# Expert passes of 32 token slots on four column tiles, and one more part of the weights loaded ahead

## The chip, the cores and the metric

One core of a Trainium2 chip runs the whole program. The metric is its time on the device in microseconds (us), launched once with all inputs in the chip's memory. TensorE does the matrix products in fp32 out of the on-chip memory (128 rows) into eight accumulator banks of 128 rows by 512 fp32. VectorE and ScalarE do the elementwise work and read the banks. SyncE (SP) issues the large DMA transfers.

## What is computed

One block with attention, a Fourier mix and a mixture of experts, and behind it two layers with other mixers and plain MLPs, for 256 tokens of width 1024. The part around the change is the mixture of experts:

```
def moe(h, w_router, b_router, w_gate, b_gate, w_up, b_up, w_down, b_down):
    logits = jnp.dot(h, w_router, preferred_element_type=jnp.float32) + b_router
    top_logit, top_idx = lax.top_k(logits, TOP_K)          # 4 of 32 experts
    gates = jax.nn.softmax(top_logit, axis=-1)
    ...
        g = jnp.minimum(xb @ w_gate[e] + b_gate[e], SWIGLU_LIMIT)
        u = jnp.clip(xb @ w_up[e] + b_up[e], -SWIGLU_LIMIT, SWIGLU_LIMIT)
        act = g * jax.nn.sigmoid(SWIGLU_ALPHA * g) * (u + 1)
        return act @ w_down[e] + b_down[e]
```

The result for each token is the sum over its four experts, weighed by the gates. Each of the 32 experts has three matrices of 1024 x 1024 fp32, 12.6 MB, 403 MB in all. How many tokens an expert gets depends on the data. For the inputs of this case the reference's router gives, from expert 0 to 31:

```
22 29 25 37 37 5 12 32 47 41 54 24 25 51 35 13 28 55 32 30 68 10 39 41 23 39 36 36 33 21 11 33
```

With 64 tokens to a pass that is one pass for each expert and two for expert 20, 33 in all. With 32 tokens to a pass, and 64 for expert 31, it is 16 experts with one pass, 14 with two, expert 20 with three, and one pass of 64 for expert 31: 48.

## The kernel before

The program has three stages, each a block in which every engine runs its own instruction list and waits on semaphores: `stage_first` (attention, Fourier mix, router), `stage_experts`, and `stage_second` (the two further layers). A stage begins when all engines have ended the one before.

**Passes.** `stage_experts` goes through a list of passes that the router has written: `m.table` holds each expert's first pass, `m.keys` and `m.gates` the slot and the gate of each token in each pass. `SLOTS` is the number of tokens to a pass, 64. A pass treats the 1024 output columns as two halves, one on the array's columns 0 to 63 and one on 64 to 127 (two column tiles), so that both halves' matmuls run side by side: the stationary operand is a 128 x 64 piece of the tokens, the moving one 512 columns of weights. TensorE's list in `one_pass` is: `expand(G)` with w_gate (8 row blocks), `gather` of the next pass's tokens by a one-hot matrix `sel`, `expand(U)` with w_up, `turn_x` (transposes of the gathered tokens), transposes of the weighed one-hot matrix `selg`, `combine` of the previous pass's result y into four accumulator banks, transposes of the activation g, `biases` for the next pass, and the contraction with w_down (8 row blocks) into bank Y. VectorE computes u and g from the banks (L1529 to L1536), ScalarE the sigmoid and the copies out of the banks (L1496 to L1507). The loop over an expert's passes (`pe.Fori`, L1465) has bounds that TensorE's sequencer reads from the table (L1296).

**Weights.** An expert's weights are six parts of 2 MB (two each of w_gate, w_up, w_down; k = 0 to 5). The buffer `ring` has ten places for parts; part 6e+k goes to place (6e+k) mod 10, and may be written when the part ten before it has been used in the last pass of its expert (`used`, waits on w_free and down_ps). SP issues the parts in that order (L1334). Ten parts, those of expert 0 and four of expert 1, are loaded in `stage_first` (`load_ahead`). Behind the last expert's parts SP issues four loads for the next stage (L1356 to L1361), and in `stage_second` w columns (L1893), the toeplitz rows (L1899) and more.

**Clock.** `keep_busy` (L136) issues matmuls without use while TensorE would wait.

Of the kernel before, what the change touches and what calls it, by code (L numbers as in the profile page):

```python
# [11 lines left out]
ALU = mybir.AluOpType  # L12
# [18 lines left out]
SLOTS = 64  # L31
# [31 lines left out]
for _name, _n in (("ident", P), ("ones", P), ("tri", QT * SEQ), ("iota", P), ("causal", QT * SEQ), ("cmpvalid", QT), ("etri", EXPERTS), ("gate16", 16), ("pad", 6),  # L63
# [8 lines left out]
def shape_constants():  # L72
# [56 lines left out]
    put("etri", (e[:, None] < e[None, :]).astype(np.float32))  # L129
    return out, buckets  # L130
# [82 lines left out]

def load_ahead(sp, m, t, e, parts):
    for k in parts:
        q, _ = expert_part(e, k)
        sp.dma_start(part_rows(m, q), expert_rows(t, e, k)).then_inc(m.part_in[q], 16)


def stage_first(nc, m, t):  # L220
# [9 lines left out]
    m.sel = m.moe.sb("sel", [P, QT, SLOTS])  # L230
    m.now = m.moe.sb("now", [2 * EXPERTS, SLOTS])
# [76 lines left out]
    modb_in = {a: m.sem(f"modb_in{a}") for a in (0, 4, 8, 16)}  # L308
    m.toeplitz_out, m.brows_in = m.lasting("toeplitz_out"), m.lasting("brows_in")
# [44 lines left out]
    gate_rows = [m.selT[SLOTS * half:SLOTS * half + EXPERTS, :, :].rearrange("e i n -> e (i n)") for half in range(2)]  # L354
# [5 lines left out]
    with nc.Block() as block:  # L360
# [10 lines left out]
        def _(sp):  # L371
# [55 lines left out]
            load_ahead(sp, m, t, 0, (4,))  # L427

        @block.tensor
        def _(pe):  # L430
# [317 lines left out]
            pe.wait_ge(more_chain, 5)  # L748
# [10 lines left out]
            pe.wait_ge(more_chain, 9)  # L759
# [5 lines left out]
            pe.wait_ge(more_chain, 10)  # L765
# [6 lines left out]
            pe.wait_ge(turned_sb, 4)  # L772
# [5 lines left out]
        def _(act):  # L778
# [192 lines left out]
            for half in range(2):  # L971
                act.copy(gate_rows[half], ps[0:EXPERTS, 4, SEQ:2 * SEQ]).then_inc(turned_sb, 1)

        @block.vector
        def _(v):
# [243 lines left out]
            v.tensor_copy(more[:, 0:1], ps[0:EXPERTS, 5, 0:1])  # L1219
            v.tensor_copy(more[:, 3:4], ps[0:EXPERTS, 5, 1:2]).then_inc(more_chain, 1)  # L1220
            v.wait_ge(more_chain, 1)
            v.tensor_scalar(more[:, 1:2], more[:, 0:1], float(SLOTS), 1.0, ALU.is_gt, ALU.add).then_inc(more_chain, 1)
            for n in range(2, SEQ // SLOTS):
                v.wait_ge(more_chain, n)
                v.scalar_tensor_tensor(more[:, 1:2], more[:, 0:1], float(n * SLOTS), more[:, 1:2], ALU.is_gt, ALU.add).then_inc(more_chain, 1)
            v.wait_ge(more_chain, SEQ // SLOTS)
            v.sem_inc(more_chain, 1)
# [6 lines left out]
            v.tensor_copy(more[:, 2:3], ps[0:EXPERTS, 5, 2:3]).then_inc(more_chain, 1)  # L1234
            v.wait_ge(more_chain, 6)
# [31 lines left out]

def stage_experts(nc, m, t):

# [1785 lines left out]
```

## Time and profile before

| | us |
|---|---|
| median of three runs (lowest, highest) | 1847.85 (1847.38, 1848.78) |
| the profiled execution | 1845.13 |
| its span | 1843.3 |
| expert passes, first to last matmul of weights | 221.4 to 1128.2 |
| `stage_second` from | 1131.15 |

The profile is of one execution and times count from the span's start. PE is TensorE's matmuls, PEld its weight loads, DVE VectorE, ACT ScalarE, POOL GpSimd; a q behind a name is that engine's sequencer. An fp32 matmul of the program appears as two records. The profile has the granted share of TensorE's full clock (2.4 GHz); its mean is 0.996. "Landing" is the time from the issue of a transfer to its last byte.

### The profile page before, as it was taken

Reading aid. Unit: us, or ns where it says so; the run is one execution under the profiler, and the core shown is the slowest. Engines: PE = TensorE matmul, PEld = TensorE weight load, DVE = VectorE, ACT = ScalarE, POOL = GpSimd, SP = SyncE. Lnnn points to the kernel's source line nnn. Section 1 sums busy time; section 2 is a strip of 40 time slices with the busy share of each in tenths; the row PEclk is TensorE's granted clock in tenths of the full one; section 3 lists DMA queues with packets and bytes.
Section 4 is the critical chain, followed back from the end, with each engine's and each line's share of the span. In section 5 each row is a group of like instructions: output and inputs, shape, how many; then the busy total and the mean of one; then the engine's idle time right before and its main releaser. Section 6 shows DMA issues by size and latency. Waiting matters only on the chain. (4 is left out here: it accounts for less than half of the span.)

```text
span 1843.3 us, 23681 instructions
## 1 busy us (share of the span) xinstructions
PE 1799.4 (98%) x9487; PEld 1003.5 (54%) x9488; DVE 605.5 (33%) x1262; ACT 371.8 (20%) x721; POOL 10.9 (1%) x14
## 2 busy tenths in 40 slices
PE   7999899999999999999999999999999999999998
PEld 6757533333333333333333335767995466699843
DVE  1854411111111011011011013544655544345555
ACT  3222411111111111111111113332220033222101
POOL 0000000000000000000000000000000000000001
PEclk9999999999999999999999999999999999999999
DMA  9996699999999999999999999432446443124452
GB/s 379 390 191 271 261 418 430 431 431 431 432 432 431 432 431 431 432 431 432 431 431 431 432 431 329 156 142 92 151 149 241 160 182 137 46 92 149 149 176 98
DMA packets 104495, 558.61 MB, mean 303 GB/s; under 512 B 17128, under 2 KB 33997, under 8 KB 78701
## 3 DMA queue, kind: packets, MB, share of 16 engines
q1 hardware_dynamic: 101876, 553.06, 74.3%
q10 hardware_dynamic: 2554, 4.63, 1.8%
q8 instruction: 47, 0.77, 0.2%
q14 instruction: 18, 0.15, 0.0%
HBM read 552.43 MB, written 5.23 MB: 303 GB/s over the span
## 5 line engine op out<-in xcount | busy, mean ns | idle before, releaser
L1402 PE MATMUL ps<-ring,xs 128*64 128x512 f32 x2112 | 465.5, 592 | 4.9 <-DMA ring<-in_w_up 2.5
L1402 PEld LDWEIGHTS ps<-ring,xs 128*64 128x64 f32 x2112 | 151.3, 137 | 307.6 <-issue 298.2
L1456 PE MATMUL ps<-ring,actT 128*64 128x512 f32 x1056 | 233.9, 595 | 0.0
L2274 PE MATMUL ps<-ring 128*128 128x512 f32 x448 | 192.8, 592 | 0.0
L1529 DVE TENSOR_SCALAR hT<-ps 128x512 f32<-128x512 f32 x33 | 22.8, 692 | 446.0 <-PE ps L1402 446.0
L1456 PEld LDWEIGHTS ps<-ring,actT 128*64 128x64 f32 x1056 | 72.9, 137 | 158.7 <-issue 136.8
L2274 PEld LDWEIGHTS ps<-ring 128*128 128x128 f32 x448 | 84.9, 190 | 105.7 <-issue 105.7
L2010 PE MATMUL ps<-hT,ring 128*128 128x256 f32 x512 | 117.9, 383 | 4.3 <-ACT hT L1654 2.9
L1531 DVE TENSOR_SCALAR hT<-ps 128x512 f32<-128x512 f32 x33 | 22.9, 693 | 263.5 <-PE ps L1402 263.5
L2010 PEld LDWEIGHTS ps<-hT,ring 128*128 128x128 f32 x512 | 94.7, 190 | 23.2 <-issue 5.9
L2228 PE MATMUL ps<-hT,ring 128*128 128x128 f32 x768 | 93.4, 275 | 0.2 <-ACT hT L1654 0.2
L2228 PEld LDWEIGHTS ps<-hT,ring 128*128 128x128 f32 x768 | 89.5, 192 | 0.5 <-ACT hT L1654 0.3
L1507 ACT COPY y<-ps 128x512 f32<-128x512 f32 x33 | 19.3, 586 | 246.5 <-PE ps L1456 246.5
L1412 PE MATMUL ps<-selT,y 64*128 64x256 f32 x544 | 67.9, 389 | 0.7 <-ACT y L1507 0.7
L1500 ACT COPY xs<-ps 128x512 f32<-128x512 f32 x33 | 19.4, 587 | 232.4 <-PE ps L1376 232.4
L1370 PE MATMUL ps<-x_sb,sel 128*64 128x512 f32 x272 | 65.7, 605 | 0.4 <-PEq L360 0.4
L2228 PE MATMUL ps<-spare,ring 128*128 128x128 f32 x512 | 62.1, 275 | 0.0
L2228 PE MATMUL ps<-sq,ring 128*128 128x128 f32 x512 | 62.1, 275 | 0.0
L2228 PEld LDWEIGHTS ps<-sq,ring 128*128 128x128 f32 x512 | 59.6, 192 | 0.0
L2228 PEld LDWEIGHTS ps<-spare,ring 128*128 128x128 f32 x512 | 59.6, 192 | 0.0
L1496 ACT ACTIVATE hT<-hT 128x512 f32<-128x512 f32 x33 | 20.8, 630 | 190.0 <-DVE hT L1529 190.0
L2192 PE MATMUL ps<-x_sb,ring 128*128 128x256 f32 x256 | 57.4, 381 | 0.9 <-ACT x_sb L1637 0.9
(455 smaller groups left out, 1812.4 us busy)
## 6 DMA issues: line engine op xcount, KB each, us to landing
ring<-in_w_gate SPq DMA_DIRECT2D x64, 2048.0 KB, 26.2
ring<-in_w_down SPq DMA_DIRECT2D x64, 2048.0 KB, 26.1
ring<-in_w_up SPq DMA_DIRECT2D x64, 2048.0 KB, 24.6
ring<-in_mlp_w SPq DMA_DIRECT2D x16, 2048.0 KB, 8.4
ring<-in_mlp_w SPq DMA_DIRECT2D x32, 1024.0 KB, 5.4
ring<-in_w_mod SPq DMA_DIRECT2D x8, 2048.0 KB, 12.2
ring<-in_odd_w_in SPq DMA_DIRECT2D x6, 2048.0 KB, 10.1
ring<-in_w_mod SPq DMA_DIRECT2D x16, 512.0 KB, 10.9
```

The costliest lines, as they stand in the source:

```text
L1370: mm = pe.matmul(ps[SLOTS * half:SLOTS * (half + 1), TURN, :], sel[:, i, :], h2[:, i, half * 512:(half + 1) * 512], start=(i == 0), stop=( ...
L1402: mm = pe.matmul(ps[SLOTS * half:SLOTS * (half + 1), bank, :], xs[:, c % 4, c // 4 * SLOTS:(c // 4 + 1) * SLOTS], weights(v, 8 * part + c) ...
L1412: mm = pe.matmul(ps[:, COMB + 2 * half + j // 2, (j % 2) * SEQ:(j % 2 + 1) * SEQ], y[SLOTS * half:SLOTS * (half + 1), j * P:(j + 1) * P], ...
L1456: mm = pe.matmul(ps[SLOTS * half:SLOTS * (half + 1), Y, :], actT[:, f % 4, f // 4 * SLOTS:(f // 4 + 1) * SLOTS], weights(v, 16 + f)[:, hal ...
L1496: act.activation(sig, g, ACT.Sigmoid, scale=ALPHA).then_inc(sig_ok, 1)
L1500: act.copy(xs[:].rearrange("p b n -> p (b n)"), ps[:, TURN, :]).then_inc(xs_sb, 1)
L1529: v.tensor_scalar(g, ps[:, G, :], LIMIT, None, ALU.min).then_inc(g_ok, 1)
L1531: v.tensor_scalar(u, ps[:, U, :], -LIMIT, LIMIT, ALU.max, ALU.min).then_inc(u_ok, 1)
L2010: mm = pe.matmul(ps[:, bank, 0:SEQ], w[:, c, at:at + P], hT[:, c, :], start=(c == 0), stop=(c == C - 1))
L2192: mm = pe.matmul(ps[:, turn.banks[k], (d % 2) * SEQ:(d % 2 + 1) * SEQ], w[c // 4][:, c % 4, d * P:(d + 1) * P], mixT[:, c, :], start=(firs ...
L2228: mm = pe.matmul(out[:, i, :], weight[:, k, i * P:(i + 1) * P], token[:, k, :], start=(opens and k == 0 and i == 0), stop=(k == 3), skip_g ...
L2274: return pe.matmul(product_bank(layer, n), token, weight, start=(c == 0), stop=(c == PAIRS - 1))
```

## The change

`SLOTS` becomes 32, `LAST_SLOTS` 64 is used for expert 31. A class `Tiling` holds what follows from the number of slots: with 32, four column tiles of 256 output columns; with 64, two of 512 as before. The stage's functions take such a tiling. The gather reads the token columns in an order that lets two transposes instead of four turn them. `combine` has 8 matmuls with 32 rows each on four row tiles, before 8 with 64 rows on two. g's transposes become 8 matmuls with the identity, and ScalarE copies actT in two halves. `turn_sel` writes to the free half of bank Y, and so waits for y. Expert 31 has a pass of its own (`last_pass`), and between expert 30 and 31 stands a gather, combine, turn and bias for the wider tiling. The router's count of passes is made by a comparison with eight thresholds and a sum. One more part, k = 4 of expert 30, is loaded in `stage_first` after rank_ps, in four transfers into rows that are idle in the expert stage (the constants' early part, `spare`, and the half of hT that g, u and the sigmoid no longer use); its place in the ring's order stays empty.

```diff
-SLOTS = 64
+SLOTS, LAST_SLOTS = 32, 64
+AHEAD = (EXPERTS - 2, 4)
+def ahead_rows(m):
+    hT = m.hT[:].rearrange("p c n -> p (c n)")
+    return m.early[:, 0:D], m.early[:, D:2 * D], m.spare[:], hT[:, D:2 * D]
...
+            sp.wait_ge(rank_ps, 1)
+            src = expert_rows(t, *AHEAD)
+            for a, row in enumerate(ahead_rows(m)):
+                sp.dma_start(row, src[:, a, :]).then_inc(m.ahead_in, 16)
...
-            for half in range(2):
-                act.copy(gate_rows[half], ps[0:EXPERTS, 4, SEQ:2 * SEQ]).then_inc(turned_sb, 1)
+            for h in range(P // SLOTS):
+                act.copy(gate_rows[h], ps[0:EXPERTS, 4, SEQ:2 * SEQ]).then_inc(turned_sb, 1)
...
+class Tiling:
+    def __init__(self, slots):
+        self.slots, self.tiles = slots, P // slots
+        self.wide = D // self.tiles
+        self.turns = self.wide // P
+    def rows(self, h):
+        return slice(self.slots * h, self.slots * (h + 1))
+    def cols(self, h):
+        return slice(self.wide * h, self.wide * (h + 1))
...
-                load(e, e % TURN_EXPERTS, last_before(sp, e - 1), last_before(sp, e))
+                parts = [k for k in range(6) if (e, k) != AHEAD]
+                load(e, e % TURN_EXPERTS, last_before(sp, e - 1), last_before(sp, e), parts)
...
+                    fours = h2[:, i, :].rearrange("p (k n a) -> p k n a", k=2, a=4)
+                    for h in range(T.tiles):
+                        c = h * T.turns
+                        mm = pe.matmul(ps[T.rows(h), TURN, 0:T.wide], m.sel[:, i, 0:T.slots], fours[:, c // 4, :, c % 4:c % 4 + T.turns],
...
-                    for half in range(2):
-                        mm = pe.matmul(ps[SLOTS * half:SLOTS * (half + 1), bank, :], xs[:, c % 4, c // 4 * SLOTS:(c // 4 + 1) * SLOTS],
-                                       weights(v, 8 * part + c)[:, half * 512:(half + 1) * 512], start=False, stop=(c == C - 1),
+                    at = c % T.turns * P + c // T.turns * T.slots
+                    for h in range(T.tiles):
+                        mm = pe.matmul(ps[T.rows(h), bank, 0:T.wide], xs[:, at:at + T.slots], weights(v, 8 * part + c)[:, T.cols(h)],
+                                       start=False, stop=(c == C - 1), skip_group_check=True)
...
+                for j in range(T.turns):
+                    for h in range(T.tiles):
+                        c = h * T.turns + j
+                        mm = pe.matmul(ps[:, COMB + c // 2, (c % 2) * SEQ:(c % 2 + 1) * SEQ], y[T.rows(h), j * P:(j + 1) * P],
+                                       selT[T.rows(h), :, :].rearrange("p i n -> p (i n)"), start=False, stop=stop, skip_group_check=True)
...
+                for a in range(4):
+                    for lane in range(2):
+                        mm = pe.matmul(ps[64 * lane:64 * (lane + 1), TURN, a * P:(a + 1) * P], g[:, a::4], ident, start=True, stop=True)
+                mm.then_inc(actT_ps, 1)
+                biases(MOST)
+                pe.wait_ge(actT_sb, i + 1)
+                contract(MOST, v, turn, ahead)
...
+            expert(0, TURNS, first_of(pe, EXPERTS - 2), last, ahead=True)
+            gather(LAST)
+            combine(MOST, False)
+            turn_x(LAST)
+            biases(LAST)
+            with pe.Fori(last, n) as i:
+                last_pass(i, 1, TURNS)
```

TensorE's list of one pass, before (names: ring holds the weights, xs the turned tokens, x_sb the tokens, hT g, u and the sigmoid; part_in are the landings of the parts; 32x256 means the output's rows and columns):

```order
L1402 MATMUL ps<-ring,xs 64x512 [waits part_in2]
L1402 MATMUL ps<-ring,xs 64x512 x7
L1402 MATMUL ps<-ring,xs 64x512 [waits part_in3]
L1402 MATMUL ps<-ring,xs 64x512 x7
L1433 REGISTER_ALU
L1376 MATMUL ps<-consts_sb,xrow 128x128 [waits e_xrow_sb]
L1438 MATMUL ps<-consts_sb,selg 128x128 [waits e_selg_ok,e_u_ok]
L1412 MATMUL ps<-selT,y 128x256 [waits e_selT_sb,e_y_sb]
L1446 MATMUL ps<-consts_sb,hT 128x128 [waits e_act_ok,e_xs_sb]
L1383 MATMUL ps<-brows,now 64x512 [waits e_selT_sb,e_now_ok]
L1456 MATMUL ps<-ring,actT 64x512 [waits part_in4,e_actT_sb]
```

The same stretch now, from expansion U to the contraction:

```order
L1433 MATMUL ps<-ring,xs 32x256 [waits part_in2]
L1433 MATMUL ps<-ring,xs 32x256 x15
L1433 MATMUL ps<-ring,xs 32x256 [waits part_in3]
L1433 MATMUL ps<-ring,xs 32x256 x15
L1407 MATMUL ps<-consts_sb,xrow 128x128 [waits e_xrow_sb]
L1440 MATMUL ps<-consts_sb,selg 128x128 [waits e_y_sb,e_now_ok,e_selT_sb,e_selg_ok,e_u_ok]
L1448 MATMUL ps<-selT,y 128x256 x8
L1497 MATMUL ps<-consts_sb,hT 64x128 [waits e_act_ok,e_xs_sb]
L1497 MATMUL ps<-consts_sb,hT 64x128 x7
L1414 MATMUL ps<-brows,now 32x256 x8
L1461 MATMUL ps<-ring,actT 32x256 [waits part_in4,e_actT_sb]
```

Twice the matmuls stand there, a half as wide; the waits for y, selT and now moved up to the transposes of selg, and g's four transposes are eight products of 64 rows. SP's list at the end of the router, where the added transfers are:

```order
L228 DMA ring<-in_w_down 128x4096 [waits h2_ok]
L443 DMA early_consts<-in_w_down 128x1024 [waits rank_ps]
L443 DMA early_consts<-in_w_down 128x1024
L443 DMA spare<-in_w_down 128x1024
L443 DMA hT<-in_w_down 128x1024
L372 UNCONDITIONAL_BRANCH
```

Before, the block ended behind the first of these rows. The four L443 rows are the part loaded ahead.

## Rows read from the trace of the kernel before

**Rows 1.** The page's head: span and instructions.

```profile
span 1843.3 us, 23681 instructions
```

**Rows 2.** Windows: stretch, length, busy (count) per engine, clock, DMA share, GB/s.

```profile
400.00:600.00 200.00, 199.04 (x1020) 76.80 (x1018) 29.68 (x71) 33.96 (x52) 0.00 (x0) 1.00 1.01 431
```

**Rows 3.** Timeline of one pass: start, duration, engine, line, operation, count.

```profile
902.43 7.09 PE L1456 MATMUL ps<-ring,actT 128*64 128x512 f32 x32
...
916.22 1.89 PE L1370 MATMUL ps<-x_sb,sel 128*64 128x512 f32 x8
...
917.93 7.04 PE L1402 MATMUL ps<-ring,xs 128*64 128x512 f32 x32
...
924.90 0.74 PE L1376 MATMUL ps<-consts_sb,xrow 128*128 128x128 f32 x4
925.02 0.69 DVE L1531 TENSOR_SCALAR hT<-ps 128x512 f32<-128x512 f32 x1 [7.89 <-PE ps L1402]
...
925.77 0.44 PE L1438 MATMUL ps<-consts_sb,selg 128*128 128x128 f32 x2
...
926.13 2.00 PE L1412 MATMUL ps<-selT,y 64*128 64x256 f32 x16
...
928.06 0.74 PE L1446 MATMUL ps<-consts_sb,hT 128*128 128x128 f32 x4
928.23 0.37 ACT L1503 COPY selT<-ps 128x256 f32<-128x256 f32 x1 [1.96 <-PE ps L1412]
...
928.75 1.09 PE L1383 MATMUL ps<-brows,now 32*64 32x512 f32 x8
...
929.77 0.65 PE L1456 MATMUL ps<-ring,actT 128*64 128x512 f32 x2
```

**Rows 4.** SP's w_down issues (ns, first and last start), landing of first and last.

```profile
L1334 SPq DMA_DIRECT2D ring<-in_w_down x62: 327/333/333, 225.1 to 1080.4; - x62
...
ring<-in_w_down SPq DMA_DIRECT2D x1, 2048.0 KB, 7.9
...
ring<-in_w_down SPq DMA_DIRECT2D x1, 2048.0 KB, 35.7
```

**Rows 5.** Timeline in `stage_first`: four column tiles of 32, L455.

```profile
32.60 3.66 PE L455 MATMUL ps<-ring 128*32 128x256 f32 x64
```

**Rows 6.** Timeline in `stage_second`: two column tiles of 64, 128 columns.

```profile
1172.12 0.39 PE L1631 MATMUL ps<-ring,nv 128*64 128x128 f32 x4
```

**Rows 7.** Timeline at the begin of the expert stage.

```profile
214.36 3.46 PE L1370 MATMUL ps<-x_sb,sel 128*64 128x512 f32 x8 [0.43 <-PEq L360]
...
221.43 7.09 PE L1402 MATMUL ps<-ring,xs 128*64 128x512 f32 x32 [1.48 <-issue]
```

**Rows 8.** L1465 on TensorE's sequencer, first expert's end: ns, first and last start.

```profile
L1465 PEldq ALU_OP  x1: 32/32/32, 244.5 to 244.5; - x1
...
L1465 PEldq FUSED_REGOPS  x1: 46/46/46, 246.3 to 246.3; - x1
```

**Rows 9.** Toeplitz issue (timeline), its landing (DMA view), its first reader.

```profile
1138.20 1.36 SPq L1899 DMA_DIRECT2D early_consts<-toeplitz  x1
...
early_consts<-toeplitz SPq DMA_DIRECT2D x1, 768.0 KB, 6.2
...
1155.83 0.42 DVE L2721 TENSOR_TENSOR ring<-ps,early_consts 128x256 f32<-128x256 f32 x1 [2.32 <-PE ps L1566]
```

**Rows 10.** Timeline at the end of the expert stage.

```profile
1128.87 2.00 PE L1412 MATMUL ps<-selT,y 64*128 64x256 f32 x16 [0.69 <-ACT y L1507]
...
1131.15 2.17 SPq L1893 DMA_DIRECT2D ring<-in_even_w_in  x2
```

**Rows 11.** Windows in the router and the stage's begin, columns as in rows 2.

```profile
203.80:207.20 3.40, 2.31 (x19) 2.04 (x19) 3.40 (x10) 0.23 (x2) 0.00 (x0) 1.00 0.04 17
207.20:210.60 3.40, 3.40 (x16) 1.86 (x14) 2.74 (x17) 0.00 (x0) 0.00 (x0) 0.50 0.68 207
...
214.00:217.40 3.40, 3.04 (x8) 0.87 (x8) 0.03 (x1) 0.00 (x0) 0.00 (x0) 0.51 0.16 53
```

More of the change, by code:

```diff
@@ L353, in stage_first @@
     base = scratch((PASSES,), EXPERTS)
[L354 removed]
+    gate_rows = [m.selT[SLOTS * h:SLOTS * (h + 1), :, :].rearrange("e i n -> e (i n)") for h in range(P // SLOTS)]
     pick = m.pick[0:EXPERTS, :]
@@ L1452, in one_pass, with contract @@
+            def contract(T, v, turn, ahead=False):
                 for f in range(C):
-                    if f % 4 == 0:
+                    if ahead and f == 0:
+                        pe.wait_ge(m.ahead_in, 64)
+                    elif f % 4 == 0:
                         arrived(v, turn, 4 + f // 4)
-                    for half in range(2):
-                        mm = pe.matmul(ps[SLOTS * half:SLOTS * (half + 1), Y, :], actT[:, f % 4, f // 4 * SLOTS:(f // 4 + 1) * SLOTS],
-                                       weights(v, 16 + f)[:, half * 512:(half + 1) * 512], start=(f == 0), stop=(f == C - 1),
-                                       skip_group_check=True)
+                    rows = ahead_rows(m)[f] if ahead and f < 4 else weights(v, 16 + f)
+                    at = f % 4 * 2 * T.slots + f // 4 * T.slots
+                    for h in range(T.tiles):
+                        mm = pe.matmul(ps[T.rows(h), Y, 0:T.wide], actT[:, at:at + T.slots], rows[:, T.cols(h)],
+                                       start=(f == 0), stop=(f == C - 1), skip_group_check=True)
@@ L1465, in expert @@
+            def expert(v, turn, first, end, ahead=False):
                 with pe.Fori(first, end) as i:
-                    one_pass(i, v, turn)
-            with pe.Fori(0, EXPERTS // TURN_EXPERTS) as turn:
+                    one_pass(i, v, turn, ahead)
+            TURNS = EXPERTS // TURN_EXPERTS
+            with pe.Fori(0, TURNS) as turn:
                 for v in range(TURN_EXPERTS):
@@ L1478, in _ @@
+            gather(LAST)
+            combine(MOST, False)
+            pe.wait_ge(xrow_sb, last + 2)
+            turn_x(LAST)
+            biases(LAST)
+            with pe.Fori(last, n) as i:
+                last_pass(i, 1, TURNS)
         @block.scalar
         def _(act):
-            for half in range(2):
-                act.dma_start(y[SLOTS * half:SLOTS * half + EXPERTS, :], t["b_down"][0][:, 512 * half:512 * (half + 1)]).then_inc(bdown_in, 16)
-            act.wait_ge(x_ps, 1)
-            act.copy(xrow[:], ps[:, TURN, :]).then_inc(xrow_sb, 1)
@@ L1491, in _, with gathered @@
-            ins.then_inc(y_sb, 1)
-            put.then_inc(selT_sb, 1)
-            n = passes(act)
-            with act.Fori(0, n) as i:
+            def gathered(T, n):
+                act.wait_ge(x_ps, n)
+                act.copy(xrow[:, 0:T.wide], ps[:, TURN, 0:T.wide]).then_inc(xrow_sb, 1)
+                act.wait_ge(xt_ps, n)
+                act.copy(xs[:, 0:T.wide], ps[:, TURN, 0:T.wide]).then_inc(xs_sb, 1)
+            for h in range(MOST.tiles):
+                act.dma_start(y[MOST.rows(h), 0:MOST.wide], t["b_down"][0][:, MOST.cols(h)]).then_inc(bdown_in, 16)
```

261 lines of the change are left out of this document (149 added, 112 removed).

## The prediction

> **What bounds the kernel now.** I read the page first: the span of the profiled execution is 1843.3 us [rows 1]. It took 1845.13 us and the median of three runs is 1847.85, so 2.7 us come on top of what I sum in its time. Then the windows of the expert stage [rows 2]: in 200 us TensorE is busy for 199.04, and the 16 DMA engines are full too, at 431 GB/s. Which of the two sets the pace has to be read from one pass and from one load.
>
> One pass [rows 3]: the contraction starts at 902.43 and the next one at 929.77, so a pass is 27.33 us. Three times 6.87 us are weights streamed (from 902.43 to the expansion's end), 1.71 the gather (916.22 to 917.93), and 4.97 the tail between the end of expansion U, 924.80, and the next contraction. 33 passes are 902 us, from 221.43 [rows 7] to 1128.0, with under 5 us of waits. One load [rows 4]: the first w_down part issued in the stage, at 225.1, landed 7.9 us later, at 233.0; the last of the stage's 182 parts, issued at 1080.4, landed 35.7 us later, at 1116.1. That is 883.1/181 = 4.88 us a part, 29.3 us an expert. So TensorE (27.3 an expert, one expert twice) and the queue (29.3, ten parts ahead) end within 12 us of each other, and cutting TensorE alone can give no more than what the queue then allows.
>
> **TensorE after the change.** The token counts in the section on the reference give 47 passes of 32 slots and one of 64. The shape of the new expansion stands in the trace: 64 records of 128x32 by 128x256 on four column tiles took 3.66 us with their last drain [rows 5], which is 0.214 for a step of four, so 16 steps are 3.43 us, half of 6.87. Pass: G 3.45, gather 0.86 (half of 1.71), U 3.43. Tail, counted from U's end by the starts of [rows 3]: VectorE starts after 0.22; its 512-wide clamp takes 0.69, ScalarE's 256-wide copy 0.37 and a 256-wide operation of VectorE 0.42 [rows 9], so u is ready at 0.68. turn_sel takes the 0.37 of now, so combine starts at 1.05. Combine is 16 records now in 2.0 us, two row tiles at a time; four row tiles of 32 should give four steps of 0.216, start to free 1.0. The third VectorE operation ends at 1.6, inside this. The transposes of g become 16 records on two column tiles: such a pair of steps takes 0.39 with its drain [rows 6], 0.109 a step, so eight are 0.9, ending near 3.2; the two half copies of actT add 0.64 (two 256-wide copies, the second overlapping by 0.1), and the biases (8 matmuls, half as wide) end at 3.7 beside them. The contraction starts at 3.93 instead of 4.97, and takes 3.48. Sum: 3.45+0.86+3.43+3.93+3.48 = **15.2 us**.
>
> The unknown is the combine: no row has four row tiles. Bounds: 0.86 for its four steps, or 1.73 if only two run together as now. I take 1.1 to 1.2, nearer to the four, since four column tiles do run four at a time [rows 5]: pass = **15.4**, bounds 15.1 and 16.3. The strided read of the gather I cost at no more than 0.1: the transposes of [rows 3] load strided weights, and four take 0.74 with a drain of 0.28, so 0.12 each against the 0.107 of an unstrided record. For this combine the Trainium skill has a figure (TensorE: Matmul & The Clock Gate, Part 3): four row tiles of K=32 measured 3.07 times faster, not 4. By it the four steps would be 1.13 us, and the pass 15.4; no row here shows it.
>
> Between experts TensorE's sequencer now loads two table values: from the loop's counter at 244.5 to the last step before the next expert's first wait at 246.3 [rows 8] that is 1.9 us with its own 0.05 and the one before the wait. In that pass the contraction ran from 241.9 to 248.8 (as in [rows 3]), so 9 of its 16 steps (3.9 us) were still queued and hide it. After the change the same queue is 4.5 steps of 0.214, about 1.0. So **1.0 us per expert** is uncovered (bounds 0.5 and 1.5). Inside an expert the 0.5 us of loop stay covered.
>
> Total: 47 x 15.4 + 31 + 27 = 782 us, against 181 parts x 4.88 = 883. The queue sets the pace, and one part fewer is 4.9 us.
>
> **Where the queue's end lands.** Start of the stage: the gather ran at the half clock (3.46 us for 8 records [rows 7], granted clock 0.51 there [rows 11]), and halves to 1.7; the table loads behind it stay. G starts at about 219.7 instead of 221.43, its first half is done 1.7 later instead of 3.4, so the first part is issued at 221.4, not 225.1. Last part: 221.4 + 7.9 + 180 x 4.88 = 1107.5. One stall: expert 20 (68 tokens, three passes) frees its first part 1.7+15.4+1.7 = 18.8 us after its last part landed, when the four parts ahead take 19.5; with the 3.0 us by which a restarted queue is late (7.9 against 4.9 [rows 4]) that is 2 us: **1109.5**, against 1116.1.
>
> Is TensorE there by then? Let L be how far it ends an expert after that expert's last part landed. It grows by passes x 15.4 + 1.0 - 29.3: by 2.5 with two passes, it falls by 12.9 with one. From expert 20 on the passes are 3, 1, 2, 2, 1, 2, 2, 2, 2, 1, 1. L after 20: 1.7+30.8 = 32.5; then 19.6, 22.1, 24.6, 11.7, 14.2, 16.7, 19.2, 21.7, 8.8, and 0.8 for expert 30, which has one part less to wait for. So it has just caught up when the last expert's parts land. From there: the last half of U lands at -9.8 (counted from the last part), takes 3.4; the old tail without its combine 4.1; first half of the contraction 3.4: 1.2 after; second half 3.4, copy, combine and stage change 3.0 (as from 1128.2 to 1131.15 [rows 10]): 7.7 to 8. I add 1 us for clock lost in waits. The next stage begins at **1118.5 instead of 1131.15: 12.6 us less**.
>
> **What follows.** The queue still has to carry the next stage's first loads behind the same last part: the toeplitz rows were issued at 1138.2 and landed 6.2 later, at 1144.4 [rows 9], 28.3 behind the last part. Moved: 1137.8. Their first reader, L2721, starts at 1155.83, 24.7 after the stage's begin, so at 1143.2: 5 us of room, and the gain is kept. The part loaded ahead goes out after rank_ps, near 207; the DMA share was 0.04 before, then 0.68, and 0.16 from 214 [rows 11]; its 4.9 us fit before 221. ScalarE's two more gate copies (0.37 each, as L1503) I cost at nothing: the spread of the table runs beside them; uncovered they are 0.7.
>
> **Forecast:** 1845.1 - 12.6 = 1832.5 for the profiled execution, **1835.5** as a median (12.4 less).
>
> **Rivals.** (a) TensorE becomes the bound. L after expert 30 is 18 passes + 10 gaps - 286.4; the last expert can take in 2.6 of it. So above a pass of 15.5 every 0.1 us costs 1.8. At 16.3 (a combine of two row tiles at a time, the upper bound) that is +14: 1850, no gain. At 15.8 +5: 1841. For it: the margin is 0.1 us a pass, and the gap between experts counts ten times. Against: 15.2 is what the measured shapes give.
>
> (b) Slower: the row tiles of 32 don't overlap at all. Combine is then 16 x 0.216 = 3.5, a pass 18.0; the end moves by 18 x 2.5 = 45, 1880. It is slower than before from a pass of 16.2 on (12.6/18 above 15.5). Against: two tiles of 64 rows overlap now [rows 3].
>
> (c) Clock. TensorE will now wait for loads: in a one-pass expert 1.7 us of work for each 4.9. The granted clock was 0.50 from 207.2 to 210.6, that is 1.2 GHz, after a stretch in which TensorE had waited and run matmuls of few columns [rows 11]. If each expert from 20 to 30 began with as long a stretch at half clock, it would cost 1.7 each, 19 us of L, 2 of which are taken in: 1853. But from 20 to 28 TensorE hardly waits, so I expect it once or twice, the 1 us above. The Trainium skill (same page, HAM oscillation) tells of a kernel whose bursts between loads all ran cold, a rule that speaks against this change; by it the one-pass experts would run cold, 3.4 us of work in 4.9, which the queue still hides, and the trace shows no such bursts.
>
> (d) The change does little more than its loads: if the faster passes only moved the waits and the next stage waited 5 us more for toeplitz than I think, 1840.
>
> **Numbers.** Forecast case (1831 to 1839): 0.58. (a) 0.22, of it 0.11 still faster, 0.07 within 0.2%, 0.04 slower. (b) 0.04, (c) 0.06 (0.02 within, 0.04 slower), (d) 0.05; more gain than 1831 (no stall, no clock loss: last part 1107.5, stage begin 1114.7, 16.5 less) 0.05. The range takes the forecast, its better side, (d) and (a) to 16.1: 1830.5 to 1848. A measurement tells 0.2% (3.7 us) from no change. Faster 0.58+0.11+0.05+0.05 = 0.79, same 0.09, slower 0.12.
>
> **What would show it.** Right: expansion and contraction in 3.43 us each, the next contraction 15.2 to 15.5 after the one before inside expert 20's second and third pass; DMA at 431 GB/s from 222 to 1109 with one dip near 810; TensorE busy about 0.85 of the stage, waiting for ring in one-pass experts; last w part landed near 1109, L1412's heir at 1116, the next stage's first DMA issue near 1118.5, and everything behind shifted alike. Wrong: combine at 2 us or more; DMA windows under 431 between 850 and 1080, which means TensorE sets the pace; a granted clock of 0.5 in dense passes; waits on toeplitz or w_kv after the stage.

## The result, and the profile after

| | before | after |
|---|---|---|
| median of seven runs each (lowest, highest), us | 1847.85 (1846.38, 1852.35) | 1854.36 (1851.69, 1856.39) |
| span of the profiled execution, us | 1843.3 | 1852.6 |
| mean granted clock | 0.996 | 0.971 |
| first w_down part of the stage issued | 225.1 | 228.6 |
| last w_down part landed | 1116.1 | 1129.7 |
| `stage_second` from | 1131.15 | 1140.39 |

The ratio is 1.0026, 95% interval 1.0015 to 1.0037: slower, by a little over the 0.2% that can be told. A second set of runs of the changed kernel gave 1.0038 (1.0024 to 1.0052). The forecast, 1835.5 with a range up to 1848.0, was wrong in sign and by 18.9 us. Behind the expert stage the time is the same: from the begin of `stage_second` to the end of the span it was 712.2 us before and is 712.2 after. All of the loss lies ahead of 1140.39.

The head of the page after, and its row of the granted clock in 40 slices:

```profile
span 1852.6 us, 40028 instructions
...
PEclk9999899999998989899989999999999999999999
```

The window that answers to [rows 2] (stretch, length, busy of PE, PEld, DVE, ACT and POOL, clock, DMA share, GB/s):

```profile
400.00:600.00 200.00, 165.52 (x2560) 92.75 (x2564) 27.81 (x90) 37.57 (x78) 0.00 (x0) 0.92 1.00 424
```

TensorE has 34 us to spare in 200 now, and the transfers, at 424 GB/s, are the bound in this stretch. So the idea of the change holds, and the pass is nearly as short as forecast. The timeline of expert 20's second pass, against [rows 3]:

```profile
807.64 3.64 PE L1433 MATMUL ps<-ring,xs 128*32 128x256 f32 x64
...
811.09 1.09 PE L1401 MATMUL ps<-x_sb,sel 128*32 128x256 f32 x16
...
812.00 3.63 PE L1433 MATMUL ps<-ring,xs 128*32 128x256 f32 x64
...
816.18 0.44 PE L1440 MATMUL ps<-consts_sb,selg 128*128 128x128 f32 x2
...
816.55 1.15 PE L1448 MATMUL ps<-selT,y 32*128 32x256 f32 x16
...
817.63 1.23 PE L1497 MATMUL ps<-consts_sb,hT 128*64 128x128 f32 x16
...
819.70 0.64 PE L1461 MATMUL ps<-ring,actT 128*32 128x256 f32 x8 [0.25 <-ACT actT L1580]
```

Expansion G starts at 807.64 and the contraction 12.06 later; with the contraction's 3.48 that is 15.54 us a pass (15.4 was forecast, 27.33 before). What went wrong lies between experts and in the queue. Who waited for whom on TensorE, over the whole program (total, times, longest):

```profile
PE ps L1433 <- issue: 49.5, 25, 7.9
PE ps L1433 <- DMA ring<-in_w_gate: 29.4, 12, 4.3
PE ps L1433 <- DMA ring<-in_w_up: 21.9, 13, 2.9
```

The waits for w_gate and w_up are those of an engine that has caught up with its loads. The first line is another thing: ahead of an expansion TensorE waits up to 7.9 us for nothing that the profile names. The w_down issues (ns; first and last start) and the landing of the first and the last, against [rows 4]:

```profile
L1362 SPq DMA_DIRECT2D ring<-in_w_down x61: 327/333/1934, 228.6 to 1092.6; - x61
...
ring<-in_w_down SPq DMA_DIRECT2D x1, 2048.0 KB, 8.1
...
ring<-in_w_down SPq DMA_DIRECT2D x1, 2048.0 KB, 37.1
```

181 parts landed between 236.7 and 1129.7: 892.9 us for 180 steps, 4.96 each, where 182 parts took 883.0 before, 4.88 each. Twice the loads paused: near 525, as TensorE freed places of the ring late behind its 6.6 us ahead of expert 10, and in expert 20's third pass, where the forecast had it:

```profile
520.00:524.00 4.00, 4.00 (x76) 2.44 (x80) 0.06 (x1) 0.33 (x1) 0.00 (x0) 1.00 0.81 340
524.00:528.00 4.00, 4.00 (x81) 2.34 (x73) 0.42 (x1) 1.74 (x3) 0.00 (x0) 1.00 0.72 238
820.00:828.00 8.00, 8.00 (x156) 4.77 (x152) 0.42 (x1) 2.29 (x4) 0.00 (x0) 1.00 0.46 158
```

Against 431 GB/s that is 0.8, 1.8 and 5.1 us lost, 7.7 in all. The landings were delayed by less. The part issued at 825.14, the first behind the pause, landed 7.4 us after the one before it, which is 2.5 over a step of 4.9; near 525 the longest step was 5.7. Its landing (DMA view):

```profile
ring<-in_w_down SPq DMA_DIRECT2D x1, 2048.0 KB, 7.5
```

**Three things to find in the trace.** First, the stage's begin. The part loaded ahead, and the first expansion, on the timeline after:

```profile
209.24 0.91 SPq L443 DMA_DIRECT2D early_consts<-in_w_down  x2
...
210.76 0.47 SPq L443 DMA_DIRECT2D hT<-in_w_down  x1
...
224.92 6.41 PE L1433 MATMUL ps<-ring,xs 128*32 128x256 f32 x64 [4.15 <-issue]
```

ScalarE issues the four loads of b_down from 216.6 on. They took 5.0 us to land, the two of before 1.9, and the same four 1.7 in the kernel, shown further on, that issues them ahead of the part (DMA view: after, before, b_down first):

```profile
y<-in_b_down ACTq DMA_DIRECT2D x4, 32.0 KB, 5.0
```

```profile
y<-in_b_down ACTq DMA_DIRECT2D x2, 64.0 KB, 1.9
```

```profile
y<-in_b_down ACTq DMA_DIRECT2D x4, 32.0 KB, 1.7
```

TensorE's sequencer waits for them (`pe.wait_ge(bdown_in, ...)`) before it enters its loop, and gets there at 223.0 (L1534 on the sequencer: ns, first and last start):

```profile
L1534 PEldq MOVE  x1: 39/39/39, 223.0 to 223.0; - x1
```

The two loads of the table only come then, and the expansion starts 1.9 us later. In the pause of 4.15 us the clock fell, and the first half of the expansion ran at the half clock, 1.2 GHz (the clock is the third number from the end):

```profile
224.90:228.40 3.50, 3.48 (x36) 1.67 (x40) 0.00 (x0) 0.00 (x0) 0.00 (x0) 0.50 0.00 0
```

Second, the step back of TensorE's loop over turns of five experts. Expert 4's last contraction and expert 5's expansion on the timeline, and the branch between them on the sequencer (ns; a row that the end of its window cuts off, like the second here, has fewer records than x64):

```profile
346.40 3.66 PE L1461 MATMUL ps<-ring,actT 128*32 128x256 f32 x64 [0.25 <-ACT actT L1580]
357.07 4.12 PE L1433 MATMUL ps<-ring,xs 128*32 128x256 f32 x44 [7.01 <-issue]
```

```profile
L1534 PEldq COMPARE_BRANCH  x1: 6173/6173/6173, 348.9 to 348.9; - x1
```

The same branch in the kernel before, between experts 9 and 10:

```profile
L1468 PEldq COMPARE_BRANCH  x1: 226/226/226, 490.9 to 490.9; - x1
```

It comes five times, before experts 5, 10, 15, 20 and 25, and takes 5.8 to 6.9 us each time, against 0.2. Third, the queue of instruction transfers, from 225 to 1130 us (DMA view: packets, MB, share), before and after:

```profile
q8 instruction: 8, 0.13, 0.1%
```

```profile
q8 instruction: 75, 1.23, 0.5%
```

TensorE's list for one turn has 690 matmul records and as many of weight loads before, 1300 of each after. With the sequencer's own that is 1475 records before (counted from 354.2 to 490.9) and 2680 after (536 an expert). Queue q14 has two small ones more in each, so the numbers below are 10 for the kernel before. The last packet of before in the loop came at 386 us; after, some twelve of 16 KB come in every turn.

### The profile page after: what moved, and what is told of

Same layout as the page of the kernel before. It is cut to its first block and busy times, and to the rows that moved or that the text cites. A ratio compares the mean times of both kernels' runs of the same rounds, so it can differ in the third digit from the quotient of the medians.

```text
span 1852.6 us, 40028 instructions
## 1 busy us (share of the span) xinstructions
PE 1689.6 (91%) x17325; PEld 1111.7 (60%) x17326; DVE 615.3 (33%) x1399; ACT 406.1 (22%) x872; POOL 10.9 (1%) x14
## 5 line engine op out<-in xcount | busy, mean ns | idle before, releaser
L1433 PE MATMUL ps<-ring,xs 128*32 128x256 f32 (+1 forms) x6080 | 388.8, 405 | 100.8 <-issue 49.5
L1433 PEld LDWEIGHTS ps<-ring,xs 128*32 128x32 f32 (+1 forms) x6080 | 206.8, 116 | 270.3 <-issue 95.2
L1461 PE MATMUL ps<-ring,actT 128*32 128x256 f32 (+1 forms) x3008 | 179.1, 383 | 20.8 <-ACT actT L1580 12.1
L1625 DVE TENSOR_SCALAR hT<-ps 128x256 f32<-128x256 f32 (+1 forms) x48 | 20.7, 430 | 456.9 <-PE ps L1433 456.9
L1461 PEld LDWEIGHTS ps<-ring,actT 128*32 128x32 f32 (+1 forms) x3008 | 93.8, 110 | 105.8 <-ACT actT L1580 28.6
L1627 DVE TENSOR_SCALAR hT<-ps 128x256 f32<-128x256 f32 (+1 forms) x48 | 20.6, 430 | 224.8 <-PE ps L1433 224.8
L1571 ACT ACTIVATE hT<-hT 128x256 f32<-128x256 f32 x47 | 19.6, 417 | 214.3 <-DVE hT L1625 214.3
L1559 ACT COPY xs<-ps 128x256 f32<-128x256 f32 (+1 forms) x50 | 19.1, 381 | 204.1 <-PE ps L1407 204.1
L1401 PE MATMUL ps<-x_sb,sel 128*32 128x256 f32 (+1 forms) x784 | 59.1, 409 | 1.0 <-ACT y L1583 0.7
L1583 ACT COPY y<-ps 128x256 f32<-128x256 f32 x47 | 17.5, 372 | 188.5 <-PE ps L1461 188.5
L1448 PE MATMUL ps<-selT,y 32*128 32x256 f32 (+1 forms) x784 | 57.9, 405 | 0.7 <-ACT y L1597 0.7
## 6 DMA issues: line engine op xcount, KB each, us to landing
ring<-in_w_mod SPq DMA_DIRECT2D x16, 512.0 KB, 10.7
```

The costliest lines, as they stand in the source:

```text
L1401: mm = pe.matmul(ps[T.rows(h), TURN, 0:T.wide], m.sel[:, i, 0:T.slots], fours[:, c // 4, :, c % 4:c % 4 + T.turns], start=(i == 0), stop=( ...
L1433: mm = pe.matmul(ps[T.rows(h), bank, 0:T.wide], xs[:, at:at + T.slots], weights(v, 8 * part + c)[:, T.cols(h)], start=False, stop=(c == C ...
L1448: mm = pe.matmul(ps[:, COMB + c // 2, (c % 2) * SEQ:(c % 2 + 1) * SEQ], y[T.rows(h), j * P:(j + 1) * P], selT[T.rows(h), :, :].rearrange(" ...
L1461: mm = pe.matmul(ps[T.rows(h), Y, 0:T.wide], actT[:, at:at + T.slots], rows[:, T.cols(h)], start=(f == 0), stop=(f == C - 1), skip_group_c ...
L1571: act.activation(sig, g, ACT.Sigmoid, scale=ALPHA).then_inc(sig_ok, 1)
L1625: v.tensor_scalar(g, ps[:, G, 0:T.wide], LIMIT, None, ALU.min).then_inc(g_ok, 1)
```

## The experiments

Each was timed in five rounds beside the kernel before on the same chip. The experiments stand on three chips, so where two changed kernels are compared, the difference of their ratios counts for more than that of their medians.

### The loop written out

```diff
-            with pe.Fori(0, TURNS) as turn:
+            for turn in range(TURNS):
                 for v in range(TURN_EXPERTS):
-                    first = first_pass(pe, bass.ds(turn * TURN_EXPERTS + (PASSES + 1 + v), 1), v)
-                    expert(v, turn, first, first_pass(pe, bass.ds(turn * TURN_EXPERTS + (PASSES + 2 + v), 1)))
+                    e = turn * TURN_EXPERTS + v
+                    expert(v, turn, first_of(pe, e), first_of(pe, e + 1))
```

> The changed kernel with TensorE's loop over turns of five experts written out, so that its list runs forward only; nothing else differs. Theory A (TensorE's list of a turn is no longer kept near the engine, and each step back to its begin costs a fetch: the branch took 6.17 us in the changed kernel, 0.22 before): the five waits of 6.6 to 7.9 us ahead of experts 5, 10, 15, 20 and 25 shrink to the 0.5 us of the other experts, expansion G of experts 20 and 25 no longer begins at half clock, the pause of the loads at 524 to 528 goes, and the program takes 4 to 6 us less than the changed kernel, about 1849. Theory B (those waits lie beside loads that TensorE would have had to wait for anyway): the waits go but the last part lands and the next stage begins within 1 us of where they do in the changed kernel, 1853 to 1855. The instruction transfers stay (the list is still fetched once for each expert), so the mean 4.91 us for a part stays under both.

Measured: 1850.92 us, ratio 1.0017 (1.0007 to 1.0027). Expert 5's expansion on the timeline:

```profile
344.25 3.66 PE L1461 MATMUL ps<-ring,actT 128*32 128x256 f32 x64 [0.25 <-ACT actT L1580]
348.28 3.66 PE L1433 MATMUL ps<-ring,xs 128*32 128x256 f32 x64 [0.37 <-issue]
```

The five waits are gone, and with them the pause of the loads near 525. By the medians it is 3.4 us less than the changed kernel; by the ratios, against its two measurements, 1.7 to 3.9 us, with intervals that overlap: less than A expected. The five waits were 35 us, so most of them had cost nothing. In both kernels experts 7, 12, 16 and 19 end 2 us behind their last part: TensorE has caught up with its loads there, and what it loses ahead of experts 5, 10 and 15 it would have waited anyway. And the end takes back a part: expert 30 now waited 2.39 us for w_up, and the half expansion behind that wait ran at the half clock:

```profile
1088.50:1090.90 2.40, 0.02 (x3) 0.00 (x0) 0.00 (x0) 0.00 (x0) 0.00 (x0) 1.00 1.00 423
1090.90:1094.30 3.40, 3.39 (x32) 1.38 (x32) 0.00 (x0) 0.00 (x0) 0.00 (x0) 0.50 0.99 424
```

The last expert ended 9.2 us behind its last part, in the changed kernel 7.7.

### b_down ahead of the part

```diff
-            sp.wait_ge(rank_ps, 1)          (in stage_first)
+            sp.wait_ge(bdown_in, 16 * MOST.tiles)          (in stage_experts, ahead of its first load)
             src = expert_rows(t, *AHEAD)
             for a, row in enumerate(ahead_rows(m)):
                 sp.dma_start(row, src[:, a, :]).then_inc(m.ahead_in, 16)
```

> The changed kernel with the part loaded ahead issued in the expert stage, behind the landing of b_down, instead of in front of it. Theory A (the b_down rows queue behind the 2 MB, TensorE's sequencer waits for them until 222.97, and the pause lets the clock fall for expansion G of expert 0): the first expansion begins near 222 instead of 224.9 and runs its first half in 1.75 instead of 3.5 us, the first part of the stage is issued near 224 instead of 228.6, and everything behind is 4.6 us earlier: about 1850. Theory B (the start doesn't matter, since the loads catch up in the pauses at 525 and 825): under 1 us less, 1853 or more.

Measured: 1850.29, ratio 1.0021 (1.0012 to 1.0031), 4.1 us under the changed kernel by the medians and 0.9 to 3.1 by the ratios. The expansion on the timeline, and its first half among the windows:

```profile
220.68 2.58 PE L1433 MATMUL ps<-ring,xs 128*32 128x256 f32 x44 [1.18 <-issue]
```

```profile
220.70:222.50 1.80, 1.80 (x36) 1.15 (x40) 0.00 (x0) 1.28 (x1) 0.00 (x0) 1.00 0.91 335
```

It starts 5.24 us after the gather, as the forecast had it (5.34); in the changed kernel it was 8.27. The first half runs at the full clock. In this profile the last part landed at 1123.5, and `stage_second` began at 1135.9.

> Both edits together. Theory A for both: their gains add, 8 to 11 us less than the changed kernel, 1844 to 1846, 1 to 4 us below the kernel before. Theory B for either: no more than the other edit alone gives.

Measured: 1848.76, ratio 1.0008 (0.9999 to 1.0017). The two gains add for the most part (5.6 of 7.5 us by the medians, 3.3 to 5.5 by the ratios), more than either alone gives, but less than the 8 to 11 that A expected, and the kernel is level with the one before, not under it.

### The length of the loop's body by itself

```diff
-            with pe.Fori(0, EXPERTS // TURN_EXPERTS) as turn:
-                for v in range(TURN_EXPERTS):
+            with pe.Fori(0, 3) as turn:
+                for v in range(10):
...
-                    expert(v, turn, first, ...)
+                    expert(v % 5, turn * 2 + v // 5, first, ...)
```

> The kernel before (64 slots, two column tiles), but TensorE's loop body holds ten experts and runs three times, instead of five experts and six times: the same instructions in the same order, a body as long as that of the changed kernel. Theory A (it is the length of the body that makes the step back dear): the branch takes about 6 us at experts 10 and 20 instead of 0.22, of which the contraction queued ahead covers 3.9 us, the instruction transfers in the stage rise from 10 to some 70, and the mean of a part rises from 4.879 to about 4.90 us. Expert 10's wait is hidden, that of expert 20 is not: 3 us more, 1851. Theory B (the dear step back comes from the narrower passes or the waits around them, not from the length): the branch stays at 0.2 us and the time is that of the kernel before.

Measured: 1855.35, ratio 1.0038 (1.0025 to 1.0051): the kernel before, with passes of 64 slots and not one matmul changed, takes about the time of the changed one. The branch between experts 9 and 10, the expansion behind the next one (expert 20), and the instruction transfers:

```profile
L1468 PEldq COMPARE_BRANCH  x1: 6108/6108/6108, 494.9 to 494.9; - x1
```

```profile
782.68 7.72 PE L1402 MATMUL ps<-ring,xs 128*64 128x512 f32 x28 [3.60 <-issue]
```

```profile
q8 instruction: 39, 0.64, 0.3%
```

So it is the length of the body that makes the step back dear. A's sum was too low. At expert 20 there are 3.6 us of wait and 1.6 of lower clock behind it. Expert 10 was not hidden either: 4.0 us of wait and 1.5 of lower clock, of which some 2.6 came back, since TensorE waited 0.9 us for parts in the stage and not 3.5. And the gather that opens the stage came at 218.1 and not at 214.4: the granted clock was 0.50 from 202.0 to 212.3, in the kernel before only from 207.2 to 210.6, for a reason that isn't known. So it is chance that the two times are near each other.

> The kernel before (64 slots) with TensorE's loop over turns written out, so that there is no step back over a long body, but the list is fetched all through the stage. Theory A (instruction transfers delay the loads by themselves): transfers in the stage rise from 10 to some 40, no branch takes over 1 us, the first to last landing of the parts takes 3 to 6 us longer than the 883.0 of the kernel before, TensorE waits longer for parts in experts 17 to 20, and the program takes 2 to 5 us more, about 1850. Theory B (the only price of a long list is the step back): the time of the kernel before, 1847.3, within 1 us.

The same kernel with the loop written out as above. Measured: 1850.89, ratio 1.0016 (1.0007 to 1.0025). No branch is dear, and still it is 2.8 us slower: 38 instruction packets instead of 10, and 887.8 us instead of 883.0 from the first landing to the last. TensorE waits for parts from expert 16 on, before from expert 18. Its instruction queue (q8 alone):

```profile
q8 instruction: 36, 0.59, 0.2%
```

A list that is fetched again and again has two prices then: the step back, 6 us each, and a load stream that is slower by about 0.5%. The second sits where the packets are. Of the 181 steps from one landing to the next, the 36 in which a q8 packet started took 5.07 us in the mean and the other 145 took 4.86; in the kernel before 7 have one and 174, at 4.87, have none. How a 16 KB packet, 0.93 us of one of the 16 engines, delays a part was not taken apart.

### What the part loaded ahead is worth

The part was taken out of the kernel with the loop written out, and then of the changed kernel itself:

> The changed kernel with the loop written out and no part loaded ahead: all 182 parts go through the ring. The b_down rows find the queue empty, as in the kernel before, and the first expansion begins near 219.5 to 220.5. The last part lands 4.9 us later than in the kernel with both edits, which has one part less. Theory A (part of what the loaded part saves is given back at the end, since TensorE and not the loads sets it there): expert 31 ends 5.6 to 6.5 instead of 9.1 us behind the last part, so the program takes 1.5 to 2.5 us more than that kernel, about 1851. Theory B (the forecast's step: one part fewer is worth its 4.9 us): 1853.6.

Measured: 1848.4, ratio 1.0004 (0.9995 to 1.0014): no dearer than with the part (1848.76). Its last part landed 3.8 us later, 1125.2 against 1121.4, but its last expert ended 5.0 us behind that instead of 9.1. Both theories had asked for more.

> The changed kernel without the part loaded ahead, the loop over turns kept: only the narrower passes and their table. The stage begins as in the kernel before (first expansion near 220 to 221, 4 us earlier than in the changed kernel, at full clock), one part more goes through the ring (4.9 us), and expert 31 ends some 4 us less behind the last part, as the run with the loop written out and no part ahead showed. Sum: 3 to 4 us less than the changed kernel, 1850 to 1851.5. If the part loaded ahead were worth its 4.9 us: 1855 or more.

Measured: 1853.47, ratio 1.0030 (1.0021 to 1.0039), level with the changed kernel, 1854.60 on the same chip. It was 2 us over A's sum. In its profile the first half of the very last contraction ran at a granted clock of 0.54 and took 5.2 us, 1.8 more than at full clock, and the end came 6.8 us behind the last part and not 5:

```profile
1126.20:1129.60 3.40, 3.40 (x14) 1.02 (x12) 0.00 (x0) 0.00 (x0) 0.00 (x0) 0.54 0.90 324
```

In the kernel with the loop written out, then, the saved 4.9 us were given back at the end (9.1 against 5.0 us). In the changed kernel they were for the most part spent at the begin: without the part the first issue came at 223.2 instead of 228.6, and the last part landed at 1128.3 instead of 1129.7 although there was one more to load. What sets the end is a row in the profile after that the forecast passed over (timeline):

```profile
1106.02 1.94 PE L1401 MATMUL ps<-x_sb,sel 128*64 128x512 f32 x8 [0.69 <-ACT y L1583]
...
1110.66 7.09 PE L1433 MATMUL ps<-ring,xs 128*64 128x512 f32 x32
...
1119.30 7.04 PE L1433 MATMUL ps<-ring,xs 128*64 128x512 f32 x32
...
1130.34 7.09 PE L1461 MATMUL ps<-ring,actT 128*64 128x512 f32 x32
```

Expert 30 ends at 1105.3; the wide gather, combine, turn and bias take until 1110.66, and expert 31, whose w_gate had landed, starts 5.35 us later. TensorE sets the end there. A part less at the end of expert 30 doesn't help it, since nothing that expert 30's expansions wait for comes earlier by it. The next edit loads another expert's part ahead:

```diff
-AHEAD = (EXPERTS - 2, 4)
+AHEAD = (4, 4)
```

(with the waits for that place of the ring lowered by one landing behind expert 4, the loop written out, and b_down first)

> As the kernel with both edits (loop written out, part loaded ahead behind b_down), but the part loaded ahead is k = 4 of expert 4 instead of k = 4 of expert 30. The loads carry the same number of parts. Theory A (with that part already there, expert 30's contraction has nothing to wait for, yet expert 29's end and the wide gather, combine and turn between expert 30 and 31, 5.35 us, push the last expert: it ended 9.1 us behind the last part instead of the 5.6 us that the parts alone ask for): expert 30 waits for its own last part again, but TensorE then has its slack back, the last expert ends 5.5 to 7 us behind the last part, and the program takes 2 to 3.5 us less, 1845.5 to 1847. Theory B (only the number of parts counts, not whose part is loaded ahead): within 0.7 us of 1848.8.

Measured: 1844.69, ratio 0.9989 (0.9980 to 0.9998), and in a second measurement 1845.25, 0.9986 (0.9977 to 0.9995). A holds, by a little more than it expected (3.5 to 4.1 us by the ratios and the medians); the last expert ended 5.0 us behind the last part. On the timeline:

```profile
1100.37 7.09 PE L1435 MATMUL ps<-ring,xs 128*64 128x512 f32 x32
...
1120.30 7.09 PE L1463 MATMUL ps<-ring,actT 128*64 128x512 f32 x32
```

> The kernel with all edits once more, beside the changed kernel and the one with two passes on one chip: 1844 to 1846, 0.05 to 0.2% under the kernel before, if the first measurement holds; the same as the kernel before (within 0.05%) if it was chance.

The first measurement held. This version is faster than both kernels, by 0.1% than the one before, and `stage_second` begins at 1130.3 in it (1131.15 before, 1140.39 in the changed kernel).

> The same, and the wide gather ahead of expert 31 doesn't wait for the copy of y (only the combine behind it does): the transition takes 4.7 instead of 5.35 us. If the transition still sets the end, 0.6 us less than the kernel of the run before; if expert 31 begins with a wait for its own parts, no change, within the 0.5 us that a comparison can tell.

Measured: 1846.14, ratio 0.9993 (0.9984 to 1.0002): no gain, and rather 1.4 us more by the medians, within what the two intervals allow. Its profile has the first half of the last contraction at a clock of 0.59, which the profile of the run before hasn't, so 0.6 us could not have been seen. Inconclusive.

### The pause of the ring

> The kernel with all edits (loop written out, part behind b_down, expert 4's part), but the router counts at most two passes for an expert, so that expert 20 leaves out its third pass (its tokens 65 to 68 get nothing from it), 47 passes in all; every load is as before. Theory A (the loads pause only once by the ring, 4 to 5 us near 810, since expert 20 frees its first part in its third pass; the rest of the stage follows the loads): the pause goes, the last part lands 4 to 5 us earlier, and the program takes 4 to 5 us less than with all edits, about 1840. Theory B (TensorE's sum of passes sets the end): 15.5 us less, 1829. Theory C (the pause is made up for elsewhere): under 1 us.

```diff
-            v.tensor_reduce(more[:, 1:2], tmp[:, 2, 0:SEQ // SLOTS], AX, ALU.add)
+            v.tensor_reduce(more[:, 1:2], tmp[:, 2, 0:2], AX, ALU.add)
```

Measured: 1843.58, ratio 0.9977 (0.9966 to 0.9988), 1.7 us under the run beside it by the medians and 3.7 by the profiles (1838.8 against 1842.5). The window around the pause, with three passes and with two:

```profile
792.00:824.00 32.00, 29.75 (x512) 17.47 (x500) 5.39 (x17) 7.69 (x16) 0.00 (x0) 1.00 0.82 340
```

```profile
792.00:824.00 32.00, 30.65 (x524) 18.80 (x520) 5.57 (x18) 7.85 (x16) 0.00 (x0) 1.00 1.01 430
```

The pause goes (by the landings it was one step of 7.8 us, 2.9 over the others), and with it up to 3.7 of the 15.5 us of a pass: B is out, and A is the nearest, though both differences are under its 4 to 5 us. The two intervals overlap, and the size is only known to within 2 us.

> The changed kernel as it is, on the same chip as the three others: 0.2 to 0.35% over the kernel before.

Measured: 1854.60, ratio 1.0038 (1.0024 to 1.0052).

## Why the prediction was wrong, step by step

The forecast put the begin of `stage_second` at 1118.5; it was 1140.39, 21.9 us later. Most of it is in two terms: the step of a part between landings, taken over at 4.88 us for a kernel whose list is fetched all the time (12.0 us), and the begin, where the part loaded ahead was costed at nothing (4.9 us). By the profile after:

| step | forecast | measured | us |
|---|---|---|---|
| gather starts | 214.36 | 216.65 | +2.3 |
| gather to first expansion | 5.3 | 8.3 | +2.9 |
| first expansion to first issue | 1.7 | 3.7 | +2.0 |
| landing of that part | 7.9 | 8.1 | +0.2 |
| pause at expert 20, from the landings | 2.0 | 2.5 | +0.5 |
| the rest of 180 steps between landings | 878.4 | 890.4 | +12.0 |
| last part to `stage_second` | 9.0 | 10.7 | +1.7 |

(21.6 in all; the rest is rounding.)

**Right.** The pass (15.54 against 15.4), the combine (1.15 with its drain; the Trainium skill's figure for four row tiles, TensorE: Matmul & The Clock Gate, Part 3, had given 1.13, and the trace agrees), the gap between two experts of one turn (0.7 us, forecast 1.0), the queue as the bound up to expert 30, the place and about the size of the ring's pause, the unchanged time behind the stage. Rivals (b) and (d) didn't come about, nor did (a) by its way, a longer pass; but TensorE was the bound of the last 30 us. (In the prediction's best case the terms give a stage begin of 1115.2, not 1114.7; nothing hangs on it.)

**The begin.** "Its 4.9 us fit before 221" was true of the queue and missed who stands behind it: the b_down loads, 128 KB, for which TensorE's sequencer waits with everything that it has still to do. [Rows 11] showed a queue almost idle from 214.0 to 217.4; the b_down issue was not among the rows, so no price was asked for it. That is 2.9 us, and the half clock behind it 1.9, as the run with b_down first shows. Of the 2.3 us of a later gather 1.5 were there before the router (the last w_down part ahead was issued at 208.87, not 207.37; in the other profiles it was anywhere from 207.2 to 208.9). The other 0.8 can't be put down to the router's longer table: from that issue to the gather it is 7.0 us before and 7.8 after, but 7.0 to 8.6 in other profiles with the new router, and 8.7 to 9.9 in the two others with the old one. So the later gather is as far as known chance, and not a part of the change.

**Between experts.** "Inside an expert the 0.5 us of loop stay covered" and 1.0 us per expert counted the table's loads, and nothing for the step back of the outer loop. The row for it was there (0.23 us before), and so was the count of instructions, which the change almost doubles. With some 6.2 us of branch, the gap ahead of experts 5, 10, 15, 20 and 25 was 6.6 to 7.9 us and not 1. The loads hide most of it; by the run with the loop written out it cost 1.7 to 3.9 us of the program. On this the Trainium skill (Runtime: NRT & Kernel Launch, Instruction fetch mechanics) has a rule that I left out: TensorE's instruction memory holds 2048 instructions, filled in blocks of 256, and a taken branch to code outside a window of two blocks stalls for a fetch. With the size of the memory the runs agree: a turn of 1475 records is not fetched again, turns of 2680 and 2950 are. With the window of two blocks they don't: the step back over 1475 records took 0.2 us. Where there was a stall, the branch took 5.8 to 7.0 us beside full DMA queues.

**The rate.** "181 parts x 4.88" took the rate of a kernel whose list stands still for one whose list is fetched all the time. The same section of the Trainium skill calls crossing into the next block mostly hidden. For TensorE that is so (no wait at one shows in the trace), for the loads it isn't: written out, the kernel before lost 4.8 us between its landings. The changed kernel shows the same split: 72 of its steps have one q8 packet and took 5.02 us in the mean, one has two and took 7.5, and those without took 4.87, the pause left out, as before. That is the most of the 12.0 us in the table; the pause near 525 is a small part.

**The end.** Two faults in one row of the sum. "It falls by 12.9 with one" is true while TensorE is far behind; nearer to its loads it waits inside the pass for w_up. With the loop written out it ended expert 24 7.2 us behind its last part, waited twice for w_up in expert 25's first pass, 2.8 and 2.9 us, and ended that expert 17.5 behind, where the forecast has 11.7 and 14.2. And the wide gather between expert 30 and 31, 5.35 us, stood in the diff and not in the sum. The first turned "0.8 for expert 30" into 4.9, the second came on top of it, and so TensorE was the bound for the last 30 us. That is why one part fewer was worth nothing where it was put, and 3.5 to 4 us at expert 4.

**The clock**, rival (c). From expert 20 on the forecast, once or twice, was right: the half clock was granted at the begins of experts 20 and 25 alone. Ahead of them it came far more often, in 15 stretches of 3.4 to 10.2 us between 223 and 763, most of them where TensorE had caught up and waited for its loads, so "the trace shows no such bursts" held for the kernel before and not for this one. Windows of the stage, after and before (the clock is the third number from the end):

```profile
222.00:1105.00 883.00, 757.59 (x12220) 436.85 (x12220) 130.19 (x421) 183.95 (x375) 0.00 (x0) 0.95 0.99 421
```

```profile
222.00:1105.00 883.00, 875.77 (x4438) 332.85 (x4436) 121.48 (x288) 149.49 (x226) 0.00 (x0) 1.00 1.00 428
```

A mean of 0.95 is about a tenth of the stage at half clock. Behind the waits of 2.4, 4.1 and 7.9 us the half expansion that followed ran at 0.50 and was 1.7 us dearer. In one-pass experts that end 2.0 us behind their last part the loads hide it; at the begin and near the end they don't.

What stays open: how an instruction packet slows the loads, why the last contraction ran at full clock in some profiles and not in others, and why the clock in the router, and with it the stage's begin, differs from profile to profile.

## What to carry to other kernels

When a change multiplies the instructions of a loop's body, count the body's records against what the engine held so far, and look at the branch that steps back: here 0.2 us became 6, and the fetching itself slowed a saturated load stream. When a transfer is put into an "idle" queue, list the small loads behind it and who waits for them. And when the bound moves from an engine to the loads, carry the sum through to the last byte's consumer: what is saved on the queue counts only while the engine has slack there.

## What the hardware showed

TensorE's step back over a loop body of 2680 or 2950 records took 5.8 to 7.0 us while the 16 DMA engines were full, over one of 1475 records 0.2 us. A 16 KB instruction packet took 0.93 us of an engine, and 28 more of them went with 4.8 us more for 181 steps of 2 MB; the steps with a packet were the longer ones, 5.07 against 4.86 us. Four 32 KB loads took 5.0 us to land behind 2 MB, and 1.7 us ahead of it. After waits of 2.4, 4.1 and 7.9 us TensorE's granted clock stood at 0.50, and the half expansion behind each took 3.4 to 3.5 us instead of 1.7.
